# The low parts of three split projections on VectorE instead of GpSimd, and squares added in three steps, in a decoder step

## What is computed

```python
def trunk(x, attend, p):
    for layer in range(2):
        if layer == 0:      # gated MLP mixer
            z = gelu(rmsnorm(x, a_norm) @ w_in); u, v = split(z)
            v = rmsnorm(v, v_norm)
            mix = (u * chunk_spatial_mix(v, w_s, b_s)) @ w_out
        else:               # dilated sliding-window attention over one shared K/V
            mix = mixer_b(rmsnorm(x, b_norm), kv, b_w_q, b_w_o, slopes, attend)
        x = x + mix
        x = x + peer(rmsnorm(x, ffn_norm[layer]), ...)
    return rmsnorm(x, final_norm)

def peer_block(h, w_q, sub_keys, u_tab, v_tab):
    q = (h @ w_q)                      # 8 heads x 2 x 128
    s = q against sub_keys             # top 16 of 128 twice, then top 16 of 256 pairs
    a = h against u_tab[expert]; coef = softmax(top) * gelu(a)
    return sum of coef * v_tab[expert]
```

## Time and profile before

| | us |
|---|---|
| median of 3 runs | 2503.99 |
| lowest, highest | 2499.71, 2510.65 |
| the profiled execution | 2500.2 |
| its span | 2498.0 |
| granted clock, mean over the span | 0.977 |

### The profile page before, as it was taken

One profiled execution on the slowest core, in us unless ns is written; L12 is line 12 of the kernel. 1 busy time (PEld: TensorE's weight loads), 2 busy tenths in 40 slices (PEclk: granted clock), 3 DMA queues, 4 the chain that ended last, 5 costly groups with the idle time before them and its releaser, 6 DMA issues.

```text
span 2498.0 us, 47140 instructions
## 1 busy us (share of the span) xinstructions
PE 2391.0 (96%) x19346; PEld 2176.9 (87%) x19346; DVE 1600.6 (64%) x3420; ACT 799.8 (32%) x1056; POOL 163.3 (7%) x122
## 2 busy tenths in 40 slices
PE   7999999999999999999999889999999999999997
PEld 3587977898999999998976478779899999999996
DVE  3132599878854874776357256997877568648743
ACT  2321311433254235324211232123423532542332
POOL 1241500000000000000032033000000000000000
PEclk9999999999999999999999699999999999999999
DMA  5233343343444444444485033334334444444441
GB/s 193 98 131 135 118 135 134 119 139 131 135 161 159 138 149 169 150 137 135 168 268 161 7 110 127 135 118 136 135 136 136 167 152 137 160 159 151 135 151 70
DMA packets 51248, 348.89 MB, mean 140 GB/s; under 512 B 6113, under 2 KB 6129, under 8 KB 11409
## 3 DMA queue, kind: packets, MB, share of 16 engines
q1 hardware_dynamic: 44928, 324.16, 38.2%
q0 software_dynamic: 6192, 22.95, 2.9%
HBM read 342.83 MB, written 4.26 MB: 139 GB/s over the span
## 4 chain that ended last, share of the span: by engine, by line
PE 92%; DVE 3%; ACT 2%; issue 1%; POOL 0%; DMA 0%; SPq 0%; DVEq 0%; ACTq 0%; POOLq 0%
PE ps L644 20%; PE ps L650 19%; PE ps L645 19%; PE ps L634 10%; PE ps L618 5%; PE ps L538 3%; PE ps L568 2%; PE ps L775 1%; ACT C_hi L1035 1%; PE ps L510 1%; PE ps L762 1%; PE ps L512 1%; PE ps L511 1%; PE ps L920 1%; PE ps L745 1%; PE ps L721 1%
## 5 line engine op out<-in xcount | busy, mean ns | idle before, releaser
L1406 DVE TENSOR_TENSOR w_lo<-ring,w_hi 128x1024 fp32r<-128x1024 f32 x448 | 544.2, 1221 | 267.7 <-ACT w_hi L1025 260.7
L1025 ACT ACTIVATE w_hi<-ring 128x1024 fp32r<-128x1024 f32 x448 | 473.1, 1057 | 636.8 <-PE ps L645 635.8
L644 PE MATMUL ps<-C_hi,w_hi 128*128 128x288 f32 x2048 | 630.8, 308 | 19.8 <-DVE C_lo L1461 19.4
L650 PE MATMUL ps<-C_hi,w_lo 128*128 128x288 f32 x2048 | 607.3, 297 | 0.0
L645 PE MATMUL ps<-C_lo,w_hi 128*128 128x288 f32 x2048 | 601.5, 294 | 0.0
L644 PE MATMUL ps<-h_hi,w_hi 128*128 128x288 f32 x1536 | 461.5, 300 | 3.3 <-DVE slots L1414 3.3
L645 PE MATMUL ps<-h_lo,w_hi 128*128 128x288 f32 x1536 | 454.9, 296 | 0.0
L650 PE MATMUL ps<-h_hi,w_lo 128*128 128x288 f32 x1536 | 453.5, 295 | 0.0
L644 PEld LDWEIGHTS ps<-C_hi,w_hi 128*128 128x128 f32 x2048 | 386.9, 189 | 25.0 <-DVE C_lo L1461 18.5
L645 PEld LDWEIGHTS ps<-C_lo,w_hi 128*128 128x128 f32 x2048 | 390.4, 191 | 0.0
L650 PEld LDWEIGHTS ps<-C_hi,w_lo 128*128 128x128 f32 x2048 | 387.2, 189 | 0.0
(11 more groups left out here) (237 smaller groups left out, 2555.7 us busy)
## 6 DMA issues: line engine op xcount, KB each, us to landing
ring<-in_U SPq DMA_DIRECT2D x128, 1024.0 KB, 4.9
ring<-in_V SPq DMA_DIRECT2D x128, 1024.0 KB, 4.9
ring<-in_peer_q SPq DMA_DIRECT2D x16, 1024.0 KB, 4.9
ring<-in_w_in_v SPq DMA_DIRECT2D x8, 1024.0 KB, 6.1
ring<-in_w_in_u SPq DMA_DIRECT2D x8, 1024.0 KB, 4.8
ring<-in_w_out SPq DMA_DIRECT2D x8, 1024.0 KB, 4.8
big<-in_cache POOLq DMA_DIRECT2D x16, 512.0 KB, 6.3
big<-in_cache POOLq DMA_DIRECT2D x16, 256.0 KB, 7.3
```

The source lines that it names most:

```text
L644: one = pe.matmul(out, w_hi[:, h % HI_SLOTS, at], hi, start=start, stop=False)
L650: return pe.matmul(out, w_lo[:, h % (2 * R), at], hi, start=False, stop=stop)
L1025: act.activation(w_hi[:, k % HI_SLOTS, :], ring[:, bl % R, (k % 2) * HBLK:(k % 2 + 1) * HBLK], ACT.Copy).then_inc(hi_made, 1)
L1406: dve.tensor_tensor(w_lo[:, n % (2 * R), :], ring[:, n // 2 % R, n % 2 * HBLK:(n % 2 + 1) * HBLK], w_hi[:, n % HI_SLOTS, :], ALU.subtract) ...
```

## The change

GpSimd's lower parts go away with their two slots. VectorE makes them instead, in place over the ring, as in the main loops, at fixed places of its list: three while v's projection runs, two around the mean of v's squares, one behind each of the three scalings of v, the rest after; for the queries three in add_chunks (chunks 4 to 6), one before and one after the wait for the root, and one with each of the query scalings 1 to 11. ScalarE makes the first three upper parts of u before v's last two evictions, and the fourth one of the queries ahead of its table load for the root. The sum of squares becomes three additions in place (4, 2 and 1 chunks), and newton has three instructions in place of four. v_ready is signalled by v's third tile as before. GpSimd's other instructions, all of them transfers, keep their order.

The core of the diff:

```diff
-HI_SLOTS, LO_SLOTS = 4, 2
+HI_SLOTS = 4
...
-            early_lower_parts(0)
-
             pool.wait_ge(v_ready, 1)
...
-                            three = pe.matmul(out, ew_lo[:, h % LO_SLOTS, at], eh_hi[:, c, :],
+                            three = pe.matmul(out, w_lo[:, h % (2 * R), at], eh_hi[:, c, :],
...
-            def norm_part(nth):
+            def norm_part(nth, e0=None):
...
+                if e0 is not None:
+                    early_upper(e0, HI_LEAD)
                 act.activation(warm[:, nth - 1:nth], ones[:, 0:1], ACT.Sqrt)
...
-            for k in range(HI_LEAD):
-                early_upper(0, k)
+                    if (fg, m) == (3, 0):
+                        for k in range(HI_LEAD):
+                            early_upper(0, k)
...
                 link(dve.tensor_tensor(tmp, r, r, ALU.mult))
-                link(dve.tensor_tensor(tmp, tmp, ms, ALU.mult))
-                link(dve.tensor_scalar(tmp, tmp, -0.5, 1.5, ALU.mult, ALU.add))
-                link(dve.tensor_tensor(r, r, tmp, ALU.mult))
-
-            def norm(nth):
+                link(dve.scalar_tensor_tensor(out=tmp, in0=tmp, scalar=-0.5, in1=ms, op0=ALU.mult, op1=ALU.mult))
+                link(dve.scalar_tensor_tensor(out=r, in0=tmp, scalar=1.5, in1=r, op0=ALU.add, op1=ALU.mult))
+
+            def early_lower(e0, k):
+
+
+                dve.wait_ge(ehi_made, e0 + k + 1)
+                dve.tensor_tensor(w_lo[:, k % (2 * R), :], ring[:, k // 2 % R, k % 2 * HBLK:(k % 2 + 1) * HBLK],
+                                  ew_hi[:, k % HI_SLOTS, :], ALU.subtract).then_inc(elo_made, 1)
+
+            def norm(nth, e0=None):
...
-                    dve.tensor_reduce(rs[:, 1, :], src[:].rearrange("p c t -> p t c"), AXX, ALU.add).then_inc(squares_added, 1)
+                    link(dve.tensor_tensor(src[:, 0:4, :], src[:, 0:4, :], src[:, 4:8, :], ALU.add))
+                    link(dve.tensor_tensor(src[:, 0:2, :], src[:, 0:2, :], src[:, 2:4, :], ALU.add))
+                    dve.tensor_tensor(rs[:, 1, :], src[:, 0, :], src[:, 1, :], ALU.add).then_inc(squares_added, 1)
+                if e0 is not None:
+                    early_lower(e0, HI_LEAD)
                 dve.wait_ge(mean_full, nth)
...
                 link(dve.reciprocal(rs[:, 2, :], rs[:, 1, :]))
+                if e0 is not None:
+                    early_lower(e0, HI_LEAD + 1)
                 newton(rs[:, 2, :], rs[:, 0, :], rs[:, 1, :])
...
                     gained_chunk(gain, c, out)
+                    if DC - 1 - HI_LEAD <= c < DC - 1:
+                        early_lower(e0, c - (DC - 1 - HI_LEAD))
...
+            for k in range(HI_LEAD):
+                early_lower(0, k)
             dve.wait_ge(v_square, 1)
...
-            last.then_inc(v_ready, 1)
+                if m == 2:
+                    last.then_inc(v_ready, 1)
+                early_lower(0, HI_LEAD + 2 + m)
+            for k in range(HI_LEAD + 5, 16):
+                early_lower(0, k)
...
                     dve.tensor_tensor(qT[:, c, :], ps[:, b, 0:T], rs[:, 2, :], ALU.mult).then_inc(dve_free, 1)
+                    if 1 <= c < 16 - HI_LEAD - 1:
+                        early_lower(e0, HI_LEAD + 1 + c)
```

More of the change, by code:

```diff
@@ L1009, in peer @@
                         early_upper(e0, c - 4)
-                norm_part(2 + 2 * layer)
-                for k in range(HI_LEAD, 16):
+                norm_part(2 + 2 * layer, e0)
+                for k in range(HI_LEAD + 1, 16):
                     early_upper(e0, k)
@@ L1256, in gained_chunk, with add_chunks @@
                 dve.tensor_scalar(out[:, c, :], xT[:, c, :], gains[:, gain, c:c + 1], None, ALU.mult).then_inc(gained, 1)
-            def add_chunks(stage, gain, before, out):
+            def add_chunks(stage, gain, before, out, e0):
                 for c in range(DC):
@@ L1295, in _ @@
                               masks[0:NSAMP].unsqueeze(1).broadcast_to((NSAMP, AG, NSAMP)), ALU.mult).then_inc(ws_ready, 1)
+            for k in range(HI_LEAD):
+                early_lower(0, k)
             dve.wait_ge(v_square, 1)
             dve.tensor_scalar(stat[:, 3:6], stat[:, 0:3], 1.0 / DAV, EPS, ALU.mult, ALU.add).then_inc(ms_ready, 1)
+            for k in range(HI_LEAD, HI_LEAD + 2):
+                early_lower(0, k)
             dve.wait_ge(root_ready, 2)
@@ L1315, in _ @@
                 dve.engine_nop().then_inc(ug_ready, 1)
-            add_chunks("wo", 1, DC, hT)
+            add_chunks("wo", 1, DC, hT, 16)
             def peer(layer):
-                norm(2 + 2 * layer)
+                e0 = 16 * (layer + 1)
+                norm(2 + 2 * layer, e0)
                 for c in range(HP):
@@ L1581, in _ @@
             dve.wait_ge(kv_saved, 16 * 3)
-            add_chunks("ob", 4, 2 * DC, gained_in_wide)
+            add_chunks("ob", 4, 2 * DC, gained_in_wide, 32)
             peer(1)
```

3 lines of the change are left out of this document (removed).

## The result

| | before | after |
|---|---|---|
| median of 7 and 7 runs, us | 2503.32 | 2484.22 |
| lowest, highest | 2499.71, 2510.65 | 2476.37, 2489.79 |
| ratio, 95% interval | | 0.9918 [0.9899, 0.9938] |
| the profiled execution, us | 2500.2 | 2484.75 |
| its span | 2498.0 | 2483.0 |

What follows compares the result with a forecast made beforehand. TensorE, busy 96% of the span, was taken as the bound, so only its waits and low clock could give time. 10.7 + 5.8 + 4.0 + 0.3 = 20.8 us off 2500.2 gave 2479.4, forecast as 2480, range 2473 to 2489.

Steps and rivals of the forecast that it cites:

- A, 10.7 us: Projection of u, from 100 us: earlier start and no waits for POOL's lower parts take back all 10.7 us lost.
- Lower parts six to eight: In u's projection, VectorE makes them by 115.5, 119.1 and 122.6; needed at 116.6, 119.8 and 123.0.
- B, 5.8 us: First layer's query projection, from 242 us: earlier mean and shorter root make the fifth half begin 5.8 us earlier.
- The rounds of 3.7 us: Second layer's query projection, before the mean: VectorE's next addition comes 3.7 us after the last, three such rounds.
- C, 4.0 us: Second layer's query projection, from 1468 us: mean 1.3 us earlier, 7.5 us from there to the fifth half; together 4.0.
- The end, 0.3: Root at the kernel's end: one step less, 0.3 us.
- the main loops are unchanged: Outside the three split projections: the main loops gain or lose nothing.
- The clock still falls: Rival: low clock stays at A's start (3 us) and in C (some 1.7 us); 2484 us, chance 0.09.
- VectorE is late in A: Rival: scaling keeps 4.45 us, lower parts come 1.0, 2.5, 5.9 late; A gives 4.8; 2485 us, chance 0.06.
- The reduction rule holds: Rival, sum of squares in B and C: three additions gain nothing, 2 x 1.6 us less; 2483 us, chance 0.06.
- VectorE's long rows are its own: Rival, all three projections: long rows aren't POOL's doing and stay; slower than before, 2502 us, chance 0.05.

Runs made afterwards that it cites:

- early_upper: Kernel before, with only ScalarE's first three upper parts of u moved before v's last two evictions; GpSimd keeps the lower parts: 2495.47 us, ratio 0.999.
- pool_in_place: early_upper, with GpSimd writing the lower parts in place over the ring, without waiting for a slot: 2504.78 us, ratio 1.0017.
- after_again: The kernel after, unaltered, run again on another chip: 2480.28 us, ratio 0.9906.
- pool_reads: Kernel after, plus sixteen unused GpSimd subtractions over spare SBUF beside each of B and C: 2493.82 us, ratio 0.9947.
- one_reduce: Kernel after, with the sum of squares as a single tensor_reduce in place of three additions: 2485.89 us, ratio 0.9937.

## Why the prediction was right

**A, 10.7 us.** Measured 10.5 (4.8 + 58.4 before, 1.4 + 51.3 after). Its two causes, the late start with the low clock and the waits for POOL's lower parts, are shown by early_upper (6.6 of it) and pool_in_place (the other 3.9). Lower parts six to eight were forecast to be made by 115.5, 119.1 and 122.6; the sixth and the seventh came at 114.2 and 117.6, and the eighth is the first of the group from 119.77, so out by 121. They came earlier since the root was out sooner (scaling begins at 110.7, not 111.9). In the rival's sum for this stage the second delay is too small: from its own numbers lower part seven would come 3.5 us late (119.1 + 4.2 against 119.8), not 2.5; its price, from part eight's 5.9, stands.

**B, 5.8 us.** Measured 6.5. Up to the mean 3.7 was forecast and 3.7 measured (10.69 to 7.01), with 0.37 for the gained chunk and 2.6 for the additions. From the mean on 7.6 us were forecast and 7.2 measured: I charged 0.5 for the lower part that stands before the mean is read, and it cost about 0.2, since it was nearly done when the mean came out (TensorE's two matmuls end at 240.86, reading begins at 241.11). The remaining 0.3 lies behind the fifth half and was not forecast.

**C, 4.0 us.** Measured 4.3. The rounds of 3.7 us came (additions at 1448.90, 1452.60, 1456.32 and 1460.02), the waits were 0.92 and 0.59 us where I had 1.2 and 0.9, and the mean came 1.4 earlier (10.80 to 9.43) for a forecast of 1.3. From the mean to the fifth half 7.5 were forecast and 7.2 measured; in the kernel before 0.30 of this was a wait for a POOL lower part, which the prediction doesn't name.

**The end, 0.3.** Measured 0.3.

**What the sum left out.** The four parts come to 21.6 us, and v's half ended 0.5 earlier, which isn't the change's: early_upper, with the old sum and root, has it too. w_out then takes 1.6 us more. The step at fault is "the main loops are unchanged", which I let stand for everything outside the three projections. The 2.48 us pause before w_out is in both kernels; in the kernel before the granted clock stayed up behind it, and in the kernel after it fell, to 0.72 to 0.78 in 169.4 to 176 us (0.74 in after_again). Why is open, and what the change has to do with it isn't shown: early_upper, where GpSimd still makes A's lower parts, has the fall too, and pool_reads, with the whole change in it, has the pause and no fall (w_out 61.9). In nine profiles with the pause two had the clock up behind it.

So there is some luck in how near the number is. The stages gave 0.8 more than their sum and w_out took 1.6 off, which leaves 20.0 of the 20.8. The medians are too coarse to confirm this: 19.1 us between those of the first runs, 24.6 between those of the later ones. And 2484.22 lies 4.2 above the forecast mostly because the forecast was counted from a profiled execution of 2500.2, 3.1 below what became the median of the kernel before.

**The rivals.** *The clock still falls*: not in A, B or C of the kernel after, where the windows show 1.00; it fell in w_out instead, so that half of this rival came true in a place that I hadn't looked at. That C kept its clock was not certain either: one_reduce, with the same first waits, lost it there. *VectorE is late in A*: no, the scalings took 2.35. *The reduction rule holds*: no. The Trainium skill, "VectorE: DVE Perf Modes", section "The perf-mode tier table", has both kinds in one tier; one_reduce has 4.25 us against 2.6, and the strided reduction was the slower one, as its row had said. *VectorE's long rows are its own*: no, by the kernel after (root steps of 0.46, the product for hT 0.51 at all its 24 places) and by pool_reads, which brings long rows back.

**Where the gain came from**, then: of 21.6 us in A, B, C and the end, 10.5 are A's place and slots, and would have come with GpSimd too; 4.5 hang on the three additions by one_reduce's profile (3.2 without its clock); the remaining 6.6 are VectorE freed of GpSimd's reads, less its own new lower parts, with the root's shorter form, which no run takes alone (it gave 0.3 at the end of the kernel). The parts don't simply add: pool_reads, with the additions and the short root kept, still gives back 10.9 us in B and C.

## What to carry to other kernels

Before work is given to GpSimd because it is idle, look at who else is in SBUF at that time: a subtraction of 2.4 us there can make a 0.16 us step of VectorE take 2.33, and VectorE doing the same subtraction itself for 1.22 us was cheaper. Where a helper engine is late, ask first whether it is slow or only short of slots and started late; here that was all of A's loss. A short pause of TensorE costs more than its length when the clock falls behind it, and here the same pause was followed by a fall in some kernels and not in others, so it is safer to take the pause out than to count on the clock.

## What the runs showed that was not expected

- Giving GpSimd more room made the kernel slower in B and C (63.2 and 66.1 us against 59.9 and 60.1): the two slots had spaced its work so that it met fewer of VectorE's steps.
- GpSimd's fill holds a VectorE row with one tensor operand (a tensor_scalar, 0.36 to 0.71 us) and lets one with two pass (0.45).
- GpSimd is held as well: its subtraction took 1.90 us alone over spare SBUF and 2.58 across VectorE's lower part, which started at 245.76 and took its 1.22.
- Stages with the same code differ by the granted clock between profiles: the prompt part 86.2 to 94.0 us, w_out 61.9 to 64.6, w_o 23.1 to 24.9. The prompt part's spread alone, 7.8 us, is more than B's whole gain; the comparison of stages told the parts apart where the medians could not.
